# One product with a matrix of ones, root and inverse of 128x512, in three of the norms of a two-block forward pass

## What is computed

```
def rms_norm(x, g):
    xf = x.astype(jnp.float32)
    y = xf * lax.rsqrt(jnp.mean(xf * xf, axis=-1, keepdims=True) + RMS_EPS)
    return (y * g.astype(jnp.float32)).astype(x.dtype)
...
        h = rms_norm(x, norm_mix[l])
        proj = h @ w_in[l]
...
        x = x + merged @ w_out[l]
        h = rms_norm(x, norm_mlp[l])
        x = x + jnp.square(jax.nn.relu(h @ w_ff1[l])) @ w_ff2[l]
    return rms_norm(x, norm_final)
```

## Time and profile before

| | us |
|---|---|
| median of 3 runs | 1529.21 |
| lowest and highest | 1528.72, 1530.65 |
| the profiled execution, its own time | 1529.55 |
| its span in the trace | 1527.7 |
| PE busy | 1499.9 (98%) |
| DVE busy | 889.2 (58%) |
| ACT busy | 776.4 (51%) |
| POOL busy | 734.3 (48%) |

### The profile page before, as it was taken

How to read it: one execution, slowest core, us unless ns; L and a number is a source line. 1 busy time by engine, 2 the same in 40 slices (tenths; PEclk the granted TensorE clock), 3 DMA queues, 4 the chain that set the end, 5 groups by cost and what they waited for, 6 DMA issues and landing times.

```text
span 1527.7 us, 19779 instructions
## 1 busy us (share of the span) xinstructions
PE 1499.9 (98%) x7395; PEld 1185.1 (78%) x7395; DVE 889.2 (58%) x1430; ACT 776.4 (51%) x1238; POOL 734.3 (48%) x463
## 2 busy tenths in 40 slices
PE   7999999999999999999999999999999999999997
PEld 6776557878888888888887787777888888888885
DVE  5568884243144774947535423522102599999998
ACT  5577885223243323242344643632224588888885
POOL 4465665544584645556454664743557351141100
PEclk9999999999999999999999999999999999999999
DMA  9120002322233564555232331121226389999984
GB/s 373 68 83 1 1 1 80 122 97 96 96 118 119 193 238 176 193 193 193 85 101 69 111 124 46 66 83 56 97 97 253 122 341 410 403 390 387 390 316 178
DMA packets 74943, 250.79 MB, mean 164 GB/s; under 512 B 11732, under 2 KB 13076, under 8 KB 74841
## 3 DMA queue, kind: packets, MB, share of 16 engines
q1 hardware_dynamic: 67264, 234.41, 41.9%
q0 software_dynamic: 4752, 8.11, 1.5%
q10 hardware_dynamic: 2824, 6.94, 1.2%
HBM read 244.94 MB, written 12.66 MB: 169 GB/s over the span
## 4 chain that ended last, share of the span: by engine, by line
PE 90%; DVE 5%; ACT 2%; DMA 1%; issue 1%; POOL 1%; SPq 0%; DVEq 0%; POOLq 0%; ACTq 0%
PE ps L449 17%; PE ps L450 17%; PE ps L453 17%; PE ps L1070 3%; PE ps L1066 3%; PE ps L1067 3%; PE ps L472 2%; PE ps L475 2%; PE ps L478 2%; PE ps L1099 2%; PE ps L1095 2%; PE ps L1096 2%; PE ps L670 2%; PE ps L508 1%; PE ps L839 1%; PE ps L648 1%
## 5 line engine op out<-in xcount | busy, mean ns | idle before, releaser
L316 POOL TENSOR_TENSOR RS<-RAW,RS 128x1024 fp32r<-128x1024 f32 x173 | 432.6, 2504 | 395.0 <-ACT RS L307 391.2
L307 ACT ACTIVATE RS<-RAW 128x1024 fp32r<-128x1024 f32 x305 | 320.3, 1056 | 233.4 <-PE ps L453 139.1
L449 PE MATMUL ps<-RH,RS 128*128 128x512 f32 x800 | 316.7, 396 | 7.8 <-ACT RS L307 7.2
L453 PE MATMUL ps<-RH,RS 128*128 128x512 f32 x800 | 312.3, 390 | 0.0
L450 PE MATMUL ps<-RH,RS 128*128 128x512 f32 x800 | 312.0, 390 | 0.0
L449 PEld LDWEIGHTS ps<-RH,RS 128*128 128x128 f32 x800 | 150.6, 188 | 42.8 <-ACT RS L307 7.2
L453 PEld LDWEIGHTS ps<-RH,RS 128*128 128x128 f32 x800 | 150.4, 188 | 32.4 <-DVE RS L316 0.8
L450 PEld LDWEIGHTS ps<-RH,RS 128*128 128x128 f32 x800 | 150.7, 188 | 31.3 <-issue 1.0
L316 DVE TENSOR_TENSOR RS<-RAW,RS 128x1024 fp32r<-128x1024 f32 x131 | 154.2, 1221 | 7.4 <-ACT RS L307 6.8
L449 PE MATMUL ps<-RA,RS 128*128 128x512 f32 x400 | 156.3, 391 | 0.0
L450 PE MATMUL ps<-RA,RS 128*128 128x512 f32 x400 | 155.7, 389 | 0.0
(11 more groups left out here) (410 smaller groups left out, 2679.6 us busy)
## 6 DMA issues: line engine op xcount, KB each, us to landing
RAW<-in_w_ff SPq DMA_DIRECT2D x64, 512.0 KB
RAW<-in_w_gate SPq DMA_DIRECT2D x45, 512.0 KB, 16.3
RAW<-in_w_up SPq DMA_DIRECT2D x43, 512.0 KB, 16.3
RAW<-in_w_down SPq DMA_DIRECT2D x42, 512.0 KB, 16.1
PB<-in_ada SPq DMA_DIRECT2D x24, 512.0 KB, 3.7
TB<-in_ada SPq DMA_DIRECT2D x24, 512.0 KB, 3.8
RAW<-in_w_gb SPq DMA_DIRECT2D x16, 512.0 KB
RAW<-in_w_ga SPq DMA_DIRECT2D x16, 512.0 KB
```

Of the source, the lines that this page charges most:

```text
L307: act.activation(RS[:, spl[n], 0, :], raws[slot[n]], ACT.Copy).then_inc(*HI.up(n))
L316: eng.tensor_tensor(RS[:, s, 1, :], raws[slot[n]], hif(RS[:, s, 0, :]), ALU.subtract).then_inc(*mark.up(n))
L449: pe.matmul(b[:, :], wh, xh, start=(k == 0), stop=False)
L453: last = pe.matmul(b[:, :], wl, xh, start=False, stop=(k == K - 1))
```

## The change

In norms 1, 2 and 3 the four matmuls of the sums and the four of the spreading are replaced by one matmul: the 128x128 matrix of ones as weights and `RST` (128x512) moving, so that the sums land on every partition at once. The root and the inverse are then taken of 128x512 in place of 128x4. Norm 2 takes no root: ACT adds epsilon to the mean square and DVE inverts that, which gives the square of the inverse root directly, so that the squaring on DVE goes. The eviction of the spread values by ACT goes in norms 1 and 2. In norm 3 the eight products on DVE read the inverse from `RST` in SBUF.

```
+        def spread_sums(key, acc, banks=ALL8):
+            pe.matmul(take(key, banks), onesf[:, :], acc, start=True, stop=True).then_inc(*P.up(key))
...
-            row_sums(("rms", 1), RST, B67)
+            spread_sums(("rms", 1), RST, B67)
...
-                spread(("rmsb", 1), ("rr", ("rms", 1)), 0, B67)
...
-                    row_sums(("rms", 2), RST, RB)
-                    spread(("rmsb", 2), ("rr", ("rms", 2)), 0, RB)
+                    spread_sums(("rms", 2), RST, RB)
...
-            row_sums(("rms", 3), RST, RB)
+            spread_sums(("rms", 3), RST, RB)
...
-        spread(("rmsb", 3), ("rr", ("rms", 3)), 0, (7,))
...
+        def spread_root(key):
+            act.wait_ge(*P(key))
+            act.activation(RST, ps[key], ACT.Sqrt, bias=small[:, 0:1], scale=1.0 / D).then_inc(*A.up(("ev", key)))
...
-                root(("rms", 1), 0)
-            elif i == 3:
-                evict(("rmsb", 1), RST)
+                spread_root(("rms", 1))
...
-                    root(("rms", 2), 0)
+                    act.wait_ge(*P(("rms", 2)))
+                    act.activation(RST, ps["rms", 2], ACT.Identity, bias=small[:, 0:1], scale=1.0 / D).then_inc(
+                        *A.up(("ev", ("rms", 2))))
...
-                    evict(("rmsb", 2), RST)
...
-                root(("rms", 3), 0)
+                spread_root(("rms", 3))
...
+        def spread_inverse(key):
+            dve.wait_ge(*A(("ev", key)))
+            dve.reciprocal(RST, RST).then_inc(*V.up(("rr", key)))
...
-                dve.wait_ge(*A(("ev", ("rmsb", 1))))
+                after(("rr", ("rms", 1)))
...
-                row_root(("rms", 1))
+                spread_inverse(("rms", 1))
...
-                    row_root(("rms", 2))
-                elif x == 1:
-                    dve.wait_ge(*A(("ev", ("rmsb", 2))))
-                    tt(RST, RST, RST, ALU.mult, "rst2")
+                    spread_inverse(("rms", 2))
...
-            elif k == 7:
-                row_root(("rms", 3))
...
-        dve.wait_ge(*P(("rmsb", 3)))
+        spread_inverse(("rms", 3))
+        after(("rr", ("rms", 3)))
         for k in range(8):
-            dve.scalar_tensor_tensor(X[:, k, :], X[:, k, :], GM_VECS(VG_FIN, k), ps["rmsb", 3], ALU.mult,
-                                     ALU.mult).then_inc(*V.up(("x2", k), ("ev", ("rmsb", 3))))
+            dve.scalar_tensor_tensor(X[:, k, :], X[:, k, :], GM_VECS(VG_FIN, k), RST, ALU.mult,
+                                     ALU.mult).then_inc(*V.up(("x2", k)))
```

More of the change, by code:

```diff
@@ L2033, in scaled_residual @@
             if u == 0:
-                after("rst2")
+                after(("rr", ("rms", 2)))
             tt(TMP[:, j, :], ps[name, u], RST, ALU.mult, ("ev", (name, u)))
```

## The result

| kernel | runs | median | lowest, highest | ratio to before, 95% interval |
|---|---|---|---|---|
| before | 20 | 1529.04 | 1527.88, 1532.16 | |
| changed | 20 | 1531.65 | 1529.74, 1532.89 | 1.0014 [1.0008, 1.0020] |

The changed kernel is 0.14% slower, about 2 us (2.6 between the medians). The forecast was 1528.4 with a range up to 1531.6: the difference has the other sign, and the median lies just above the range. The profiled execution took 1530.99, with a span of 1529.2 (before: 1527.7).

A forecast was written before the change was run, and what follows sets the result against it. PE's own instruction stream was taken to bound the kernel, with DVE the limit for a while at norm 1. Terms +1.9, -1.78 and -0.92 gave -0.8 on 1529.55, 1528.75; 0.34 lower for the median, 1528.4, range 1526.9 to 1531.6.

The forecast's parts named there:

- the first rival: Norm 1, ahead of the gates' transposes: PE's clock falls in the new wait of 4.1, giving 1530.0; chance 17%.
- The price: Cost of PE's clock falling in norm 1's new wait ahead of the gates' transposes: +1.5 to +1.7.
- The sum: All three norms together: 1.9 - 1.78 - 0.92 = -0.8 on the profiled execution's 1529.55.
- Norm 1, step by step: Norm 1: the long inverse starts `blocks(10)` 3.5 later, part is won back at POOL's L316, net cost +1.9.
- The slope: Norm 1's inverse, from rows of 4 and 16 elements: 6.2 ns per element above 0.155, so 3.35 for 512.
- the lower bound's +0.6: Norm 1's cost if the inverse runs at plain speed, 0.71: +0.6, total 1527.1; as a rival, 8%.
- Any length from 2.0 to 4.4 gives the same: Norm 1: an inverse of 2.0 to 4.4 costs the same +1.9, since DVE meets the same L316.
- Norm 2: PE from the sums to the second dense matmul takes 1.09 for 2.87, a gain of 1.78 that stays.
- the cover: Norm 2: POOL's half of the fifth feed-forward tile ends near 487.9, PE wants it at 489.7; 1.8 to spare.
- The long inverse waits for POOL: Norm 1: the inverse waits for four L316 to end, so norm 1 costs +6.8, total 1533.3; chance 8%.
- Norm 3: PE's spreading goes, -0.92; DVE's eight products take 0.6 to 3 more, ending between 851 and 854, at no cost.
- What was to show: Changed profile: from 60 to 470 everything 1.9 later, behind norm 2 about 0.1 later, behind norm 3 about 0.8 earlier.

The follow-up runs named there:

- norm 1 alone: Only the norm 1 hunks of the diff applied to the kernel before, norms 2 and 3 as before: 1533.29, ratio 1.0029.
- memsets first: The changed kernel with DVE's two memsets set ahead of norm 1's long inverse: 1529.27, ratio to before 0.9998.
- plain product: The changed kernel with norm 1's long inverse replaced by one plain-speed product, so it doesn't compute the reference: 1528.94, ratio to before 0.9996.
- inverse twice: The changed kernel with norm 1's inverse taken twice, so it doesn't compute the reference: 1534.31, ratio to before 1.0035, 5 runs.
- the filled kernel: The changed kernel with four unused fp32 matmuls of 128x512 on PE ahead of its wait for the gates' sigmoid: 1528.20, ratio to before 0.9995.
- norms 2 and 3: Only norms 2 and 3 changed against the kernel before, norm 1 as before: 1527.32, ratio 0.9984.
- norm 2 alone: Only norm 2 changed against the kernel before: 1528.69, ratio 0.9993.
- The three kernels with fillers: Unused matmuls ahead of the gates' transposes: four in the changed kernel (1528.20), four with only norm 1 changed (1531.40), one with only norms 2 and 3 changed (1526.35).
- norm 3 alone: Only norm 3 changed against the kernel before: 1529.63, ratio 1.0001.
- The changed kernel, again: The changed kernel without further edits, timed a second time beside the kernel before: 1531.70, ratio 1.0014.

## Why the prediction was wrong

**The step that failed** is the first rival: "PE's clock falls in the new wait (17%)". The forecast's sum let TensorE stand idle for 4.1 and put nothing against it; the clock fell behind that wait. Of the 14 profiled executions, the six with a wait of 2.45 to 5.40 ahead of the transposes (the changed kernel twice, norm 1 alone, memsets first, plain product, inverse twice) all have the fall there, and the eight with 2.00 or less have not. The argument against it, "1.28 of idle time left the clock alone", was read from a wait a third as long. The other row at hand, pointed the other way: PE had idled and run small transposes there, as it does here. The kernel before shows at that place:

```profile
115.11 0.70 PE L636 MATMUL ps<-M,X 64*128 64x256 f32 x2 [1.03 <-ACT TMP L1197]
115.94 4.33 PE L648 MATMUL ps<-identf,PB 128*128 128x128 f32 x20
```

No wait there was longer than 1.03, less than the 1.28 that did no harm at the gates. So the length of the wait alone doesn't say whether the clock falls, and a short harmless wait was no proof for a long one.

**The price** was +1.5 to +1.7. In the profiled execution it was 1.58, in the second one of the same kernel 2.24 (63.45 - 61.21), in the kernel with the memsets first 2.74. Over all runs, filling the wait gave 3.5 in the whole change and 1.9 in norm 1 alone. So the price for one fall was right for the shortest kind only. (By the ratios the fillers gave 2.9 and 2.6.)

**The sum** of -0.8 was right: 1.84 - 1.76 - 0.92 = -0.84. On the 1529.04 to 1529.60 of before that gives 1528.2 to 1528.8, and the filled kernel, which has the change and not the fall, took 1528.20. With a fall of 1.6 to 2.7 it is 1529.8 to 1531.5, and the median was 1531.65. That the sum comes out to a few hundredths has luck in it, by the spread of "to a" and of the falls elsewhere.

**Norm 1, step by step.** The product costs what four columns did (right). The slope of 6.2 ns an element gave 3.35 for the inverse, and it took 3.35, 3.35 and 3.33; the estimate of 4.4 that stood beside it was too long by 1. DVE meets POOL's L316 as worked out (4.08 for 4.1), and the lower bound's +0.6 was +0.6 with the plain product. "Any length from 2.0 to 4.4 gives the same" was not tried as such; two inverses gave 2.3, not 3.35, more. That PE would stand idle for 4.1 was nearly right (3.81); that it costs nothing was not.

**Norm 2.** PE's 2.87 became 1.10, as worked out (1.09), and the cover was near the 1.8 forecast: POOL's half ended at 489.29 + 2.64 = 491.93, and the forecast's 487.9 for it and 489.7 for PE's need are 491.8 and 493.6 when shifted by the 3.91 that norm 2 starts later here.

**The long inverse waits for POOL** (8%) did not happen: 3.35 beside L316 in norm 1, and 3.33 in norm 3.

**Norm 3.** The eight products were given 0.6 to 3 on top of 5.4 and took 10.15, 4.8 more. In the terms of before they ended at 855, where 851 to 854 was forecast. It was hidden all the same, so only the size was off. The Trainium skill (SBUF — State Buffer, on the shared port pair) says that a DVE operation with two SBUF inputs and a GpSimd one that reads SBUF exclude each other. The trace agrees: with the inverse moved from PSUM into SBUF the products took 10.15 beside three L316, for 5.36 before, when L316 ran beside them as well.

**What was to show** behind norm 1: "everything 1.9 later" from 60 to 470 was 3.4 later near 111 (114.51 for 111.09), 2.15 later in place of 0.1 behind norm 2 (824.03 for 821.88), and 2.1 later in place of 0.8 earlier behind norm 3 (869.30 for 867.18). A granted clock under 1 near 50 was named there as what would make the prediction wrong, and that it was.

**What stays open.** The falls near 120, 828 and 1208 come and go between kernels whose programs are the same up to there: norms 2 and 3 has one near 825 and norm 2 alone, which differs only from norm 3 on, has none. Each costs 0.7 to 0.9 (d to e: 14.0 to 14.2 with it, 13.3 without), 1.0 to 1.5 (b to c: 366.8 to 367.3 for 365.8) or about 1.5 (f to end: 661.3 to 662.3 for 659.8 to 660.8). The three kernels with fillers that leave 0.31 of waiting or less have no fall near 120, and those of memsets first and plain product have none either, so no rule can be read from it. Filling the wait gained 3.5 on the whole change by the medians and 2.9 by the ratios, each of which is uncertain by 0.0006 to 0.0009, or 0.9 to 1.4. The fall behind the wait explains 1.6 to 2.7 of it, so within the noise nothing else is needed. An estimate from the clock comes to the same: 0.0020 of mean clock (0.9965 for 0.9945) over a span of 1529 is 3.1, and 0.0019 in norm 1 alone is 2.9. Whether the part above 2.7 is real, and then that fall lasting longer in more runs or the others coming more often in the changed kernel, can't be told from one profile for each.

## What to carry to other kernels

A delay that makes an engine wait longer can cost more than the wait itself: in a kernel whose TensorE is busy 98% of the time, look at the wait's new length as well as at its end, and at every place in the trace where the granted clock already falls. A wait longer than any that the trace has there is not covered by one that did no harm. When a change pays in some places and costs in one, time the places apart: here two of three norms gave 2.3 us and the third took more than that away. If a wait before dense work can't be shortened, matmuls whose result nobody reads may keep the clock up: here four of them took the changed kernel from 1531.7 to 1528.2, and the transposes behind them started no later (51.46 for 51.72). That was in a wait of 3.8; in one of 1.3 a filler showed no gain.

## What was not expected of the hardware

- The clock after a wait is not the same from one execution to the next. The changed kernel, again, in windows of PE:

```profile
49.00:51.00 2.00, 0.00 (x0) 0.70 0.00 0
51.00:53.00 2.00, 1.35 (x6) 0.50 0.00 0
53.00:55.00 2.00, 2.00 (x7) 0.50 0.00 0
55.00:57.00 2.00, 2.00 (x7) 0.59 0.00 0
```

  The wait is as long as in the first execution (3.82 for 3.81), but the clock falls inside it and not behind it, and is at 1.2 GHz until near 57: 0.7 more lost. The Trainium skill (TensorE: Matmul & The Clock Gate, Part 1) says of the slow matmuls at a kernel's start that their number differs from run to run of one kernel, and the trace agrees for those behind a wait: the starts 0.43 apart last from 52.89 to 55.88 in the first execution, and here until near 56.6.
- Fp32 matmuls of 128x512 lie 0.86 apart, worked out from 3.59 for four and 1.02 for one (to their modelled end), for 0.23 of a dense fp32r one.
- A stall between DVE and POOL can go either way by a hair. Before, POOL's L316 started 3.06 after the first of the 16 additions and held up one of the last (5.72 together). In norm 3 alone, with the same program there, L316 started 3.06 after the first addition as well:

```profile
36.91 3.26 DVE L1763 TENSOR_SCALAR PB<-PB,PE 128x62 f32<-128x62 f32 x16
39.97 2.47 POOL L316 TENSOR_TENSOR RS<-RAW,RS 128x1024 fp32r<-128x1024 f32 x1 [2.66 <-ACT RS L307]
```

  But the additions took 3.26, and PE had no wait at all ahead of the gates' transposes.
